# Layer 2 of a two-layer trunk: raw X transposed once for two norms, weights at the copies, row scales behind the projections

## What is computed

```python
def rmsnorm(x, g):
    return x * lax.rsqrt(jnp.mean(x * x, axis=-1, keepdims=True) + EPS) * g

for l in range(2):
    h = rmsnorm(x, mix_norm_g[l])
    mk, mv = split(rmsnorm(mem, mem_norm_g[l]) @ w_mem_kv[l])
    if l == 0:
        q, k, v, fl, qm = split(h @ w_in_a[0])            # forgetting attention, 12 heads
    else:
        qd, qm = split(h @ w_q_b[0])                      # rotary on qd; differential attention
        # heads read shared_k1, shared_k2 (rotary), shared_v
    y_mem = softmax(qm @ mk.T * HEAD_DIM ** -0.5) @ mv    # 4 heads
    x = x + concat(y_self, y_mem) @ w_out[l]
    h = rmsnorm(x, ffn_norm_g[l])
    x = x + (swiglu(h) if l == 0 else moe_swiglu(h))      # dense, then top 2 of 8 experts
    if l == 0:
        kd, vs = split(rmsnorm(x, kv_norm_g) @ w_kv_shared)
return rmsnorm(x, final_norm_g)
```

## Time and profile before

| what | value |
|---|---|
| median of three plain runs | 1425.39 us (1425.25 to 1425.84) |
| the profiled execution's own time | 1424.84 us |
| span from its first to its last instruction | 1423.1 us |
| granted TensorE clock, mean | 0.998 |
| busy: PE, weight loads, DVE, ACT, POOL | 99%, 84%, 80%, 67%, 4% |
| moved by DMA | 439.95 MB, 309 GB/s over the span |

### The profile page before, as it was taken

The page is one execution under the profiler, slowest core; times in us unless marked ns, Lnnn a source line. Parts: engine busy times, 40 slices in busy tenths (PEclk is TensorE's granted clock), DMA queues, the critical chain, the costliest instruction groups (busy, mean ns, idle before and its releaser), DMA issues.

```text
span 1423.1 us, 20481 instructions
## 1 busy us (share of the span) xinstructions
PE 1405.4 (99%) x7646; PEld 1199.2 (84%) x7646; DVE 1144.0 (80%) x1032; ACT 953.2 (67%) x878; POOL 51.9 (4%) x81
## 2 busy tenths in 40 slices
PE   8999999999999999999999999999999999999997
PEld 8988999998988888888888888888888888888885
DVE  6686544447786999888888888888889898888997
ACT  6556433346466777777777777777777777777775
POOL 2100000002001000000000000000000000000100
PEclk9999999999999999999999999999999999999999
DMA  9753655554526999999999999999999999999993
GB/s 316 247 171 121 205 186 195 181 178 159 182 90 255 376 379 377 372 387 380 379 373 377 382 371 379 390 370 378 377 383 381 376 376 377 377 393 357 323 369 122
DMA packets 207564, 439.95 MB, mean 309 GB/s; under 512 B 7309, under 2 KB 54433, under 8 KB 207506
## 3 DMA queue, kind: packets, MB, share of 16 engines
q1 hardware_dynamic: 202912, 423.65, 82.1%
q0 software_dynamic: 4576, 15.51, 3.1%
q10 hardware_dynamic: 18, 0.01, 0.0%
HBM read 433.36 MB, written 5.78 MB: 309 GB/s over the span
## 4 chain that ended last, share of the span: by engine, by line
PE 93%; DVE 3%; ACT 1%; DMA 1%; POOL 0%; SPq 0%; issue 0%; ACTq 0%; DVEq 0%
PE bank L1966 29%; PE bank L1968 29%; PE bank L1967 29%; PE bank L2669 2%; DMA raw<-in_w_in_a_dram 1%; DVE wlo L1156 1%; PE bank L2179 1%; ACT whi L714 1%; PE bank L2576 0%; PE bank L2229 0%; PE bank L2210 0%; PE bank L2070 0%; DVE hn L1190 0%; PE bank L2564 0%; PE bank L1981 0%
## 5 line engine op out<-in xcount | busy, mean ns | idle before, releaser
L1156 DVE TENSOR_TENSOR wlo<-raw,whi 128x2048 fp32r<-128x2048 f32 x396 | 903.4, 2290 | 177.4 <-ACT whi L714 175.9
L714 ACT CAST whi<-raw 128x2048 fp32r<-128x2048 f32 x396 | 756.2, 1914 | 201.9 <-PE bank L1968 195.7
L1966 PE MATMUL bank<-whi,op_hi 128*128 128x512 f32 (+1 forms) x1160 | 438.0, 378 | 2.4 <-DVE op_lo L1548 1.5
L1968 PE MATMUL bank<-whi,op_lo 128*128 128x512 f32 (+1 forms) x1160 | 430.2, 371 | 0.0
L1967 PE MATMUL bank<-wlo,op_hi 128*128 128x512 f32 (+1 forms) x1160 | 429.7, 370 | 0.0
L1966 PEld LDWEIGHTS bank<-whi,op_hi 128*128 128x128 f32 x1160 | 218.6, 188 | 44.0 <-DVE wlo L1156 4.2
L1968 PEld LDWEIGHTS bank<-whi,op_lo 128*128 128x128 f32 x1160 | 218.5, 188 | 38.2
L1967 PEld LDWEIGHTS bank<-wlo,op_hi 128*128 128x128 f32 x1160 | 218.7, 189 | 35.3
L1966 PE MATMUL bank<-whi,h2T_hi 128*128 128x512 f32 x544 | 213.9, 393 | 1.0 <-DVE h2T_lo L1597 0.6
L1968 PE MATMUL bank<-whi,h2T_lo 128*128 128x512 f32 x544 | 211.9, 390 | 0.0
L1967 PE MATMUL bank<-wlo,h2T_hi 128*128 128x512 f32 x544 | 211.9, 389 | 0.0
(11 more groups left out here) (343 smaller groups left out, 805.4 us busy)
## 6 DMA issues: line engine op xcount, KB each, us to landing
raw<-in_w_gate_up_moe_dram SPq DMA_DIRECT2D x223, 1024.0 KB, 7.3
raw<-in_w_down_moe_dram SPq DMA_DIRECT2D x109, 1024.0 KB, 7.4
raw<-in_w_gate_up_dense_dram SPq DMA_DIRECT2D x22, 1024.0 KB, 5.1
raw<-in_w_down_dense_dram SPq DMA_DIRECT2D x11, 1024.0 KB, 5.0
raw<-in_w_in_a_dram SPq DMA_DIRECT2D x10, 1024.0 KB, 12.2
raw<-in_w_out_dram SPq DMA_DIRECT2D x8, 1024.0 KB, 4.9
raw<-in_w_kv_shared_dram SPq DMA_DIRECT2D x6, 1024.0 KB, 5.1
raw<-in_w_q_b_dram SPq DMA_DIRECT2D x4, 1024.0 KB, 5.3
```

The lines of the kernel that those rows point to most:

```text
L714: a.copy(whi[:, c % SPLIT, :], src).then_inc(hi_ready, 1)
L1156: d.tensor_tensor(wlo[:, c % SPLIT, :], src, whi[:, c % SPLIT, :].bitcast(F32), ALU.subtract).then_inc(lo_ready, 1)
L1966: m.matmul(dst, sh, mh, start=start and i == 0, stop=False)
L1968: last = m.matmul(dst, sl, mh, start=False, stop=stop and i == n - 1)
```

## The change

In layer 2 X itself is transposed once, without scale or weight, into banks 4 to 7, chunk c in bank 4 + c//2. The row scale commutes with the projection and is applied behind it; the weights lie along the contraction and become a [P,1] column for each chunk, applied as ACT and DVE copy out of the banks. The chunks are copied one by one: for kv 2 x 8 copies of 128 columns (one set for each tile), for mix 8 of 256 columns, on each of the two engines. The order of the projections is now kd, vd, qd, qm, into banks 0 to 3. kd, vd and qd get the row scale when they are taken. qm does not: its scores lack the row scale, which `max1` applies to the row maximum and `exp1` as the scale of the exponential.

`load_gain(4, ...)`, the products on POOL, `apply_gain` for both norms and ACT's scalings go. Two loads of columns (`head_g`) are new, behind the router's. The changed order, engine by engine:

```diff
-        + [("kd", 0), ("qd", 0), ("vd", 0), ("qm", 1)]
+        + [("kd", 0), ("vd", 0), ("qd", 0), ("qm", 1)]
...
-    return 4 + (p - P_M1 if p < P_KV else (p - P_KV) % 3)
+    if p < P_KV:
+        return 4 + p - P_M1
+    return p - P_KV if p < P_KV + 4 else 4 + (p - P_KV) % 3
```

POOL's queue:

```diff
+                for i, g1 in enumerate((kv_norm_g, mix_norm_g[1])):
+                    pool.dma_start(head_g[:, i, :], g1.rearrange("(k p) -> p k", p=P)).then_inc(router_in, 16)
...
-            pool.dma_start(mix_gain, mix_norm_g[1:2, :].to_broadcast([P, D])).then_inc(mix_gain_in, 16)
-            load_gain(4, 12)
...
-            for n, dst, g1 in ((4, hn, gain[:]), (5, tok, mix_gain)):
...
-                    g.tensor_tensor(dst[:, 1, cols], X[:, 1, cols], g1[:, cols], ALU.mult).then_inc(kv_gained, 1)
...
-            load_gain(6, 18)
+            load_gain(6, 12)
```

ACT:

```diff
+                    row = stat[:, 4, 3, t:t + 1] if SETS1[g][0] == "mem" else 1.0
                     ins = a.activation(pr[:, c0:c1], b[:, c0:c1], ACT.Exp, bias=negm[:, S1 + g, t:t + 1],
+                                       scale=row, accum_out=rsum[:, S1 + g, t:t + 1])
...
+            def kv_fill_hi(t):
+                for c in range(KC):
+                    act.wait_ge(tr_ready, 16 + 4 * t + c // 2 + 1)
+                    c0 = SEQ * (c % 2) + P * t
+                    ins = a.activation(op_hi[KV_BUF][:, c, P * t:P * (t + 1)], bank[4 + c // 2][:, c0:c0 + P], ACT.Copy,
+                                       scale=head_g[:, 0, c:c + 1])
+                    if c % 2:
+                        ins.then_inc(fill_hi, 1)
+            def mix_fill_hi():
+                for c in range(KC):
+                    act.wait_ge(fill_lo, int(FILL[4]) + 4 + c // 2 + 1)
+                    c0 = SEQ * (c % 2)
+                    ins = a.activation(op_hi[MIX_BUF][:, c, :], bank[4 + c // 2][:, c0:c0 + SEQ], ACT.Copy,
+                                       scale=head_g[:, 1, c:c + 1])
+                    if c % 2:
+                        ins.then_inc(fill_hi, 1)
...
             sqrt_table()
             for q in range(2):
                 sum_squares(q, x_added, 0)
+            act.wait_ge(router_in, 64)
+            kv_fill_hi(0)
             split_hi(U_KV + 1)
+            for q in range(2, 4):
+                sum_squares(q, x_added, 0)
+            kv_fill_hi(1)
+            for t in range(NT):
+                norm_sqrt(4, t)
+            mix_fill_hi()
             a.activation(warm[:], warm[:], ACT.Exp)
             for u in range(2, 6):
                 split_hi(U_KV + u)
```

DVE:

```diff
+                elif what == "vd":
+                    ins = d.tensor_tensor(v[:, :, cols], b2, stat[:, 4, 3, :].unsqueeze(2).to_broadcast([P, NT, WIDE]),
+                                          ALU.mult)
...
                 else:
-                    ins = d.tensor_scalar(head_cols(p), b2, SCALE, None, ALU.mult)
+                    row = stat[:, 4 + (what == "qd"), 3, :]
+                    ins = d.tensor_tensor(head_cols(p), b2, row.unsqueeze(2).to_broadcast([P, NT, WIDE]), ALU.mult)
...
+                if SETS1[g][0] == "mem":
+                    step(ins)
+                    ins = d.tensor_tensor(negm[:, S1 + g, :], negm[:, S1 + g, :], stat[:, 4, 3, :], ALU.mult)
                 ins.then_inc(rowmax, 1)
...
+            def head_scales():
                 dve.wait_ge(norm_std, norm_count(4, 1))
+                step(d.reciprocal(stat[:, 4, 3, :], stat[:, 4, 2, :]))
+                d.tensor_scalar(stat[:, 5, 3, :], stat[:, 4, 3, :], SCALE, None,
+                                ALU.mult).then_inc(head_scale_ready, 1)
...
             ffn_h2_lo(FFN_STEPS - 1)
-            split_lo(U_KV)
             add_tile(0)
             add_tile(1)
+            split_lo(U_KV)
             norm_mean(4, 0, 2)
-            norm_scale(4, 0)
-            for n in (4, 5):
-                for h in range(2):
-                    apply_gain(n, X, 4, 0, h)
+            kv_fill_lo(0)
             add_tile(2)
-            tile_fill_lo(4, 0)
             add_tile(3)
             split_lo(U_KV + 1)
-            tile_fill_lo(5, 0)
             norm_mean(4, 1, 2)
-            kv_scale()
-            tile_fill_lo(4, 1)
-            tile_fill_lo(5, 1)
+            kv_fill_lo(1)
+            head_scales()
+            mix_fill_lo()
             split_lo(U_KV + 2)
             take(18)
             rotate(18, 1)
             split_lo(U_KV + 3)
             take(19)
-            rotate(19, 2)
             split_lo(U_KV + 4)
             take(20)
             heads_T(0)
+            rotate(20, 2)
             split_lo(U_KV + 5)
```

PE:

```diff
+            def tile_transposes(t):
+                pe.wait_ge(x_added, 2 * t + 2)
+                if t:
+                    pe.wait_ge(fill_lo, int(FILL[4]) + 4)
+                for c in range(KC):
+                    c0 = SEQ * (c % 2) + P * t
+                    last = m.transpose(bank[4 + c // 2][:, c0:c0 + P], X[:, t, P * c:P * (c + 1)], ident[:])
+                    if c % 2:
+                        last.then_inc(tr_ready, 1)
...
             for t in range(NT):
                 ffn_down(FFN_STEPS - 2, 0, 0, parts=(t,))
-                ffn_down(FFN_STEPS - 1, 0, 0, final=True, parts=(t,),
-                         between=(lambda: tile_transposes(4, 0)) if t else None)
...
-            tile_transposes(5, 0)
-            pe.wait_ge(fill_lo, int(FILL[4]) + 2)
+                if t:
+                    tile_transposes(0)
+                ffn_down(FFN_STEPS - 1, 0, 0, final=True, parts=(t,))
+            pe.wait_ge(fill_lo, int(FILL[4]) + 4)
             project(18, (0,))
-            pe.wait_ge(fill_lo, int(FILL[4]) + 4)
+            tile_transposes(1)
             project(19, (0,))
-            tile_transposes(4, 1)
-            tile_transposes(5, 1)
-            for p in (18, 19):
-                pe.wait_ge(fill_lo, int(FILL[4]) + 4 + 2 * (p - 17))
-                project(p, (1,))
+            pe.wait_ge(fill_lo, int(FILL[4]) + 8)
+            project(18, (1,))
+            project(19, (1,))
+            pe.wait_ge(fill_lo, int(FILL[5]))
             project(20)
             heads_T(0)
             project(21)
```

More of the change, by code:

```diff
@@ L912, in applied_act @@
                     mem_pair_hi(h // 2)
-            def tile_fill_hi(n, t):
-                for h in range(2):
-                    act.wait_ge(tr_ready, 16 + 4 * t + 2 * (n - 4) + h + 1)
-                    a.copy(op_hi[FILL_BUF1[n - 4]][:, 4 * h:4 * h + 4, t * P:(t + 1) * P],
-                           bank[TR_BANK1[n - 4][t] + h][:].rearrange("p (c n) -> p c n", c=4)).then_inc(fill_hi, 1)
+            def kv_fill_hi(t):
[14 more added lines that the diff above has]
+                        ins.then_inc(fill_hi, 1)
             def ffn_silu(j, turns=0):
@@ L1182, in apply_gain @@
                     dve.wait_ge(mem_gain_in, 16)
-                elif n == 5:
-                    dve.wait_ge(mix_gain_in, 16)
-                else:
-                    dve.wait_ge(gain_in, 16 * (n - 2 if n < 5 else n - 3))
-                dst = tok if n == 5 else hn
+                else:
+                    dve.wait_ge(gain_in, 16)
                 cols = slice(512 * h, 512 * (h + 1))
-                g = bank[6 + h][:] if n == 1 else mix_gain[:, cols] if n == 5 else gain[:, cols]
-                d.scalar_tensor_tensor(out=dst[:, t, cols], in0=src[:, t, cols], scalar=stat[:, of, 3, t:t + 1],
+                g = bank[6 + h][:] if n == 1 else gain[:, cols]
+                d.scalar_tensor_tensor(out=hn[:, t, cols], in0=src[:, t, cols], scalar=stat[:, of, 3, t:t + 1],
                                        in1=g, op0=ALU.mult, op1=ALU.mult).then_inc(hn_ready, 1)
@@ L1541, in head_pair_lo, with kv_fill_lo, mix_fill_lo @@
                                 op_hi[KV_BUF][:, 2 * pr:2 * pr + 2, :].bitcast(F32), ALU.subtract).then_inc(fill_lo, 1)
-            def tile_fill_lo(n, t):
-                hi, lo = op_hi[FILL_BUF1[n - 4]], op_lo[FILL_BUF1[n - 4]]
-                for h in range(2):
-                    dve.wait_ge(fill_hi, int(FILL[4]) + 4 * t + 2 * (n - 4) + h + 1)
-                    d.tensor_tensor(lo[:, 4 * h:4 * h + 4, t * P:(t + 1) * P],
-                                    bank[TR_BANK1[n - 4][t] + h][:].rearrange("p (c n) -> p c n", c=4),
-                                    hi[:, 4 * h:4 * h + 4, t * P:(t + 1) * P].bitcast(F32),
-                                    ALU.subtract).then_inc(fill_lo, 1)
+            def kv_fill_lo(t):
+                for c in range(KC):
+                    dve.wait_ge(fill_hi, int(FILL[4]) + 4 * t + c // 2 + 1)
+                    c0, cols = SEQ * (c % 2) + P * t, slice(P * t, P * (t + 1))
+                    ins = d.scalar_tensor_tensor(out=op_lo[KV_BUF][:, c, cols], in0=bank[4 + c // 2][:, c0:c0 + P],
+                                                 scalar=head_g[:, 0, c:c + 1], in1=op_hi[KV_BUF][:, c, cols].bitcast(F32),
+                                                 op0=ALU.mult, op1=ALU.subtract)
```

(33 more changed lines are left out.)

47 lines of the change are left out of this document (11 added, 36 removed).

## The result

| | before | after |
|---|---|---|
| median, us | 1425.55 (1425.25 to 1425.84, 4 runs) | 1436.33 (1435.89 to 1437.17, 4 runs) |
| the profiled execution: time, span | 1424.84, 1423.1 | 1435.98, 1434.2 |
| granted TensorE clock, mean | 0.998 | 0.997 |

The ratio is 1.0074, with a 95% interval of 1.0062 to 1.0086: the changed kernel is 10.8 us slower. The forecast was 1424.5, with a range of 1422.6 to 1426.8; the time lies 9.5 us above the range.

A forecast was written before the change was run, and what follows sets the result against it. The prediction took TensorE (PE), busy 99% of the span, as the bound. A gain of 1.95 us at the seam and a loss of 1.0 at the memory heads gave 1425.39 - 0.95, rounded to 1424.5 us, range 1422.6 to 1426.8.

The forecast's parts named there:

- POOL and its queue: Products leave POOL's seam work, two column loads of 0.91 us come near 61 us: free, 3.5 us to spare.
- the sum: Whole kernel: -1.95 us at the seam plus 1.0 at the memory heads, -0.95 us.
- the three rivals: No new wait before unit 20 (chance 0.07); memory heads cost nothing (0.15); small copies do not overlap (0.2).
- The third rival: Seam: ACT's small copies follow at full durations, unit 20 begins at 352.5, kernel 1.5 us slower, 1426.9 us; chance 0.2.
- something on top: Whole kernel: an unnamed addition lifting the third rival over 1428.2 us; chance 0.04.
- the bounds that the prediction names: Seam and heads terms together: -2.35 + 0.45 = -1.9 to -0.75 + 1.4 = +0.65 us.
- Transposes and the two waits: Seam on PE: 16 of 32 transposes go, 1.65 us, and both waits for DVE's low parts, 0.83 and 0.69 us.
- Copies: Seam fills: ACT copies 0.25 us apart at 128 columns, 0.36 at 256; DVE's 0.26 and 0.41.
- The rival of copies that don't overlap: Seam: ACT's copies take full durations, 0.49 us at 256 columns, about 0.39 at 128; 1426.9 us, chance 0.2.
- The new wait: Seam: PE stands from 348.4 to about 350.05 us for unit 20's low part, beginning it 1.95 us earlier than before.
- The heads: Layer 2's memory heads: row scaling of maxima and exponentials loses 1.0 us by the third head's transposes.
- The first rival: Seam: ACT and DVE reach unit 20 by 348.4, so no new wait; -2.9 us, 1422.4 us, chance 0.07.

The follow-up runs named there:

- e1: The changed kernel with head_g allocated behind all other tiles: 1425.11 us, 0.9991 of before; stages (layer 0's attention end to layer 2's) 311.0 us against 311.8.
- e8: e1 without the product on the row maximum and without the scale operand in the memory exponentials: 1424.44 us (one execution), stages 310.1 us.
- e9: e1 with unit 20's cast ahead of the second kv fill on ACT and its subtraction ahead of the mix fill on DVE: 1423.38 us, 0.9981 of before.
- e2: The kernel before with an unused tile of 64 bytes a partition allocated ahead of prob: 1435.76 us, ratio 1.0065 to before.
- e13: The kernel before with 64 unused bytes ahead of h2T_hi and 192 behind it, so within 256 bytes only h2T_hi moves: 1436.37 us.
- e11: The kernel before with 64 unused bytes ahead of whi and 192 behind wlo, so within 256 bytes only these weights move: 1423.18 us.
- e15: e9 with the row scale moved onto qm, op_hi0 and op_lo0 moved 192 bytes within 256, op_lo0 and op_hi1 swapped: 1418.57 us, 0.9951 of before.
- e17: e15's shift with the four op tiles in their old order, an unused tile ahead of each: 1418.74 us, 0.9949 of before.

## Why the prediction was wrong, step by step

**The step that failed** is the last of the part on POOL and its queue: "The expert stage is the same code and PE-bound, so it shifts whole." It is the same code and PE-bound, and its 1344 down products run at 0.2335 us where they ran at 0.2270: 8.7 us, and 1.6 more in the dense feed-forward. The prediction took `head_g` for two loads on an idle queue and nothing else; where its 64 bytes push the tiles behind it was not asked. In the sum no term stood for the pitch of a product whose instruction doesn't change, and none of the three rivals had it. The third rival, the slower side, was a mechanism in the seam and reached 1426.9; "something on top" had 0.04. The ends of the range are also each 0.4 to 0.5 us wider than the bounds that the prediction names for them (1425.39 - 1.9 - 0.4 = 1423.1 and 1425.39 + 0.65 + 0.4 = 1426.4); against a miss of 9.5 us that decides nothing.

**The rest of the sum held**, as e1 shows, in which only that term is missing:

- *Transposes and the two waits*: 16 transposes from X, no wait for a low fill: right.
- *Copies*: forecast 0.25 us apart at 128 columns and 0.36 at 256; measured eight in 2.18 (0.26) and eight in 3.08 (0.37). DVE 0.26 and 0.40 apart, forecast 0.26 and 0.41. The rival of copies that don't overlap falls.
- *The new wait*: forecast 1.7 us (348.4 to 350.05), measured 1.81 and, in e1, 1.83. Unit 20 begins 23.54 us behind the last down step in e1 (326.62 to 350.16), 25.37 before: -1.83, forecast -1.95. In after it is 23.73, -1.64; the 36 slower down products between (36 x 6.5 ns = 0.23) cover the difference.
- *The heads*: forecast 1.0 us at the third head's transposes. They come 52.95 us behind the last down step in e1, 53.79 before: -0.84. So 1.83 - 0.84 = 0.99 is lost on the way; e8, which leaves the scaling out, gives 0.9. How the 1.0 splits between the two turns was not measured. PE's wait rose to 1.24 in after, forecast 1.2. The product takes 0.16 us (forecast 0.15). The scale operand lengthens an exponential from 0.47 or 0.48 to 0.56 us, some 0.09, within the 0.06 to 0.11. The first of them in ACT's timeline, before and then after:

```profile
369.35 0.48 ACT L867 ACTIVATE prob<-bank,negm 128x256 f32<-128x256 f32 x1 [9.39 <-DVE negm L1475]
```

```profile
370.38 0.56 ACT L860 ACTIVATE prob<-bank,negm,stat 128x256 f32<-128x256 f32 x1 [9.59 <-DVE negm L1478]
```

- *POOL*: two loads of 0.91 us each, and the idle time ahead of the third decay load fell from 5.33 to 3.58, the 3.5 to spare that were forecast. Free.
- *The sum*: forecast -0.95; e1's stages give -0.9, its median -0.97, which with its interval is all but level with before.
- *The first rival* (-2.9: the wait doesn't come) did not happen in the change, but e9 makes its condition true. Its stages are 2.8 us shorter than before's.

The Trainium skill, "TensorE: Matmul & The Clock Gate", section "Step-by-step: what each phase is for", says that the array reads stationary and streaming operand through two ports of their own, and that loading the next weights takes no read bandwidth from the running matmul. By that rule e2 would be level with before. It was 1.0065 of it, and moving one operand's tile (h2T_hi in e13) changed the pitch of products whose shapes and counts stayed. The measurement decides: in this kernel the pitch is not independent of where the two operands' tiles lie against each other. Whether the ports themselves have a part in it no run shows.

**Open.** What happens in the memory or the array is not shown. That the pitch is the old one again at 256 and 512 bytes and hangs on neighbouring products too suggests reads that meet, but this is only argued: no row names it. Why e11's dense products reach 0.1139 and those of e15 and e17, with the same distance from op to weights within 256 bytes, 0.1175 is not settled; nor why h2T forward by 64 and the weights forward by 64 cost different amounts. h2T's own distance to op, which e11 keeps and e2 changes, was not varied alone and may have a part of e2's 6.5 ns; nor were 96, 160, 192 or 224 bytes tried for h2T alone.

## What to carry to other kernels

In a kernel that is bound by PE, a new tile is also a shift of every tile behind it: allocate new small tiles last, and compare the mean duration of unchanged products between two profiles before looking for a cause in the code. If unchanged products differ by a few ns each, pad the old kernel by the same bytes; that one run separates the place from the change. Then treat the place as something to tune, by stage, in steps under 256 bytes: here some 4 us, against the 0.9 us of the edit. Allocating last was safe here because all large tiles already lay at multiples of 256 bytes from the weights.

## What the hardware showed unexpectedly

- The pitch of 512-column products in single precision is 0.227 or 0.2335 us, at the same granted clock (0.997 and 0.998), by the place of the stationary operand's tile against the others: 32, 64 and 128 bytes off are slow, 256 and 512 are not. For 256-column products with the weights stationary it lay between 0.1139 and 0.1200 us, and there the layout that is best for 512 columns was the slowest.
- The weight loads of the h2T blocks keep their mean of 188 ns while the products slow down (before, after, e2).
- A product is slowed by its neighbours' operands too (e13: h2T_lo under whi, both at their old places within 256 bytes, 0.2332 against 0.2270).
